# Query and key tiles of an attention layer: products for norm and rotation one gap later, two gaps in every tile, conditioning spread thinner

## The reference, cut to what matters

```python
mod = c_act @ ada_w[i] + ada_b[i]                     # conditioning
sh1, sc1, gt1, sh2, sc2, gt2 = jnp.split(mod, 6, axis=-1)
h = _modulate(_rms(x, norm1_g[i]), sh1, sc1)
...
qkv = h @ w_in
q, k, v = jnp.split(qkv, [ATT_Q_DIM, ATT_Q_DIM + ATT_KV_DIM], axis=-1)
...
q = _rope(_rms(q, q_g).astype(jnp.float32), cos, sin) * (ATT_HEAD_DIM ** -0.5)
k = _rope(_rms(k, k_g).astype(jnp.float32), cos, sin)
...
p = jnp.exp(scores - m)
p = p / (p.sum(axis=-1, keepdims=True) + jnp.exp(sink - m))
o = jnp.einsum('bnhgqk,bnkhd->bnqhgd', p.astype(vb.dtype), vb).reshape(b, s, ATT_Q_DIM)
```

## Time and profile before

| | us |
|---|---|
| median of 3 runs (3039.64 to 3040.81) | 3040.3 |
| the profiled execution | 3037.79 |
| its span, first to last instruction | 3036.0 |
| TensorE busy | 2671.8 (88%) |
| VectorE busy | 1683.7 (55%) |
| ScalarE busy | 930.1 (31%) |
| GpSimd busy | 1242.4 (41%) |
| landing of one qk weight after its issue, median | 5.0 |

### The profile page before, as it was taken

One profiled execution on the slowest core, in us unless ns is written; L12 is line 12 of the kernel. 1 busy time (PEld: TensorE's weight loads), 2 busy tenths in 40 slices (PEclk: granted clock), 3 DMA queues, 4 the chain that ended last, 5 costly groups with the idle time before them and its releaser, 6 DMA issues. The chain is left out here.

```text
span 3036.0 us, 48379 instructions
## 1 busy us (share of the span) xinstructions
PE 2671.8 (88%) x20064; PEld 2192.0 (72%) x20064; DVE 1683.7 (55%) x2078; ACT 930.1 (31%) x1551; POOL 1242.4 (41%) x630
## 2 busy tenths in 40 slices
PE   1787888999999999899996677887789999999999
PEld 1565666888877788677775576776777888878887
DVE  6754545765535543567762788788525543434434
ACT  2435333222223222255442222222234222222221
POOL 2432244444445344443432333334255444444443
PEclk9989998999999999999997888888999999999999
DMA  6421233355522233266675333333142233332333
GB/s 238 160 77 41 84 106 130 134 197 174 172 93 97 84 104 97 84 163 167 156 183 126 83 76 94 70 79 84 35 153 84 97 97 98 97 91 90 104 97 125
DMA packets 299000, 343.31 MB, mean 113 GB/s; under 512 B 214560, under 2 KB 214688, under 8 KB 298784
## 3 DMA queue, kind: packets, MB, share of 16 engines
q1 hardware_dynamic: 298784, 340.23, 37.5%
HBM read 298.29 MB, written 40.89 MB: 112 GB/s over the span
## 5 line engine op out<-in xcount | busy, mean ns | idle before, releaser
L709 POOL TENSOR_TENSOR wl<-w,wh 128x1024 fp32r<-128x1024 f32 x367 | 905.3, 2472 | 1281.2 <-ACT wh L750 1281.1
L180 PE MATMUL ps<-hi,wh 128*128 128x512 f32 x2208 | 883.4, 400 | 22.0 <-ACT qk_raw L787 10.4
L181 PE MATMUL ps<-lo,wh 128*128 128x512 f32 x2208 | 869.1, 394 | 0.0
L182 PE MATMUL ps<-hi,wl 128*128 128x512 f32 x2208 | 868.9, 394 | 0.0
L750 ACT ACTIVATE wh<-w 128x1024 fp32r<-128x1024 f32 x367 | 386.9, 1056 | 706.6 <-DMA w<-in_ffn_w_in 526.1
L1021 DVE SCALAR_TENSOR_TENSOR xt<-ps,mod,xt 128x512 f32<-128x512 f32 x384 | 286.7, 750 | 415.8 <-PE ps L182 407.6
L180 PEld LDWEIGHTS ps<-hi,wh 128*128 128x128 f32 x2208 | 420.4, 190 | 124.7 <-issue 33.8
L181 PEld LDWEIGHTS ps<-lo,wh 128*128 128x128 f32 x2208 | 420.7, 191 | 89.9 <-issue 3.7
L182 PEld LDWEIGHTS ps<-hi,wl 128*128 128x128 f32 x2208 | 420.0, 190 | 90.2
L1026 DVE TENSOR_TENSOR act<-ps,silu 128x512 f32<-128x512 f32 x88 | 60.9, 692 | 459.5 <-PE ps L182 459.5
L180 PE MATMUL ps<-act_hi,wh 128*128 128x512 f32 x704 | 282.3, 401 | 18.3 <-DVE act_lo L1030 10.7
(11 more groups left out here) (221 smaller groups left out, 3389.7 us busy)
## 6 DMA issues: line engine op xcount, KB each, us to landing
w<-in_ffn_w_in SPq DMA_DIRECT2D x176, 512.0 KB, 3.7
piece<-in_ada_w SPq DMA_DIRECT2D x96, 512.0 KB, 4.9
w<-in_ffn_w_out SPq DMA_DIRECT2D x88, 512.0 KB, 3.7
w<-in_w_rkv SPq DMA_DIRECT2D x48, 512.0 KB, 3.9
scratch<-silu SPq DMA_DIRECT2D x48, 256.0 KB, 2.9
scratch<-act SPq DMA_DIRECT2D x48, 256.0 KB, 3.1
w<-in_wqk SPq DMA_DIRECT2D x20, 512.0 KB, 5.0
xt<-in_xT SPq DMA_DIRECT2D x4, 2048.0 KB, 9.9
```

The costliest lines, as they stand in the source:

```text
L180: pe.matmul(out, w_hi(k), x_hi(k), start=first and k == 0, stop=False)
L181: pe.matmul(out, w_hi(k), x_lo(k), start=False, stop=False)
L182: ins = pe.matmul(out, w_lo(k), x_hi(k), start=False, stop=last and k == kc - 1)
L709: pool.tensor_tensor(wl[n % NW][:, :, :], wr[n % NW][:, :, :], wh[n % NW][:, :, :].bitcast(F32), ALU.subtract).then_inc(*wlo.up)
```

## The change

A few lines of the function that lays out the attention layer are changed.

```diff
                 else:
                     head, root, rest = norms[1]
-                    plan.side = joined(spread(head, 6) + [root] + spread(rest, 2), spread(plan.ada_steps(2, 4, 3), 3))
+                    plan.side = joined(spread(head, 3) + [root] + spread(rest, 1), spread(plan.ada_steps(2, 4, 3), 2))
                 for n in range(QCH + KCH):
                     j = (QCH + n) % (QCH + KCH)
-                    if n and plan.side:
-                        plan.side[0] = aux() + plan.side[0]
-                    elif n:
-                        plan.side = [aux()]
-                    plan.tile("qk", h, j, [plan.slot("wqk", j)], cuts=(3, 6) if h else (4,))
+                    if n:
+                        plan.side += [[]] * (2 - len(plan.side))
+                        plan.side[1] = aux() + plan.side[1]
+                    plan.tile("qk", h, j, [plan.slot("wqk", j)], cuts=(3, 6))
                     if h:
                         plan.between()
```

## The result

The changed kernel takes 3042.41 us (median of 20 runs, 3037.58 to 3049.46) against 3039.50 for the kernel before (20 runs): ratio 1.0014, 95% interval 1.0008 to 1.0020. So it is 2.9 us slower, inside the range, on the other side of the forecast of 3.4 us faster.

The account below looks back on a forecast made before the run. VectorE, slowed by GpSimd, was taken to bound the first half, a closed chain across engines the second. First half -4.0 and second half +0.6 gave -3.4 against the 3040.3 median: 3036.9, said as 3037; range 3030 to 3043.

Parts of the forecast that it names:

- First half, -4.0: First half of query and key tiles: v tiles begin at 184.8 instead of 188.8; bounds -12 and -1.
- Leg A: First half, to the start of tile 5: norm's matmul goes from 108.28 to 109.4, tile 5 begins at 119.5.
- Leg B: First half, tile 5 to tile 8: VectorE sets it, loses 7.9 us to GpSimd; tile 8 starts at 160.7.
- rival 1: First half: GpSimd's instructions hold VectorE for their full length, 10.9 us lost; total -0.4, 3039.9; chance 0.18.
- The 0.85: First half: VectorE loses 0.85 us for each us of GpSimd's work it meets, read from a stretched pair of pieces.
- The closed chain, 14.03 to 13.43: Second half's tile time: attention output's remainder, 0.60, leaves the chain; six turns gain 3.6 us.
- The clock, 1.8: Second half: 2.5 us waits ahead of transposes lower TensorE's clock in three tiles of six, costing 1.8 us.
- The entry, +2.4: Second half's first such tile: matmuls and value products run ahead of the products, so the chain starts 2.4 us later.
- The exit, 0: Second half, at the last weighing: TensorE has its fill of work again, no wait moves on, no cost.
- Rival 2: Engines meet in half of GpSimd's work (-4.0) and the clock stays full (-1.8): total -9.2, 3031.1; chance 0.27.
- Rival 3: First half: every conditioning piece meets GpSimd and takes 2.8 us; total +6.9, 3047.2; chance 0.07.
- Rival 4: First half: products of tiles 3 and 5 go behind a conditioning product; two waits of 1.3 us; no own chance.

Follow-up runs that it names:

- second half filled: Kernel with only the second half changed, plus six unread small products in TensorE's wait ahead of the transposes of units 1 to 6; 3.1 us over before.
- values first: Kernel before, with the second half's products of squares and rotation put behind the value products of their gap; 5.8 us under before.
- second trace of before: Kernel before, unchanged, traced a second time; no time of its own given, 362.1 us on the "whole" stretch against 361.8 in the first trace.
- second half alone: Changed kernel's second half with the first half of the kernel before; 2.7 us over before, ratio 1.0002 to 1.0019.
- first half alone: Changed kernel's first half with the second half of the kernel before; 2.9 us under before, ratio 0.9983 to 1.0000.
- after, held: Changed kernel, with GpSimd's remainder held at the entry until two units' maxima are done and at the exit until the last weighing; 1.9 us over before.
- values first, remainder late: Changed kernel's first half; second half's products at the first gap behind value products, GpSimd's remainder behind its tile's weighing and maxima; 3019.7 us, 20.0 under before.
- remainder late: Kernel before, with GpSimd's weight remainder in the second half put behind the weighing and maxima of its tile; 16.0 us under before.

## Why the prediction was wrong

**First half, -4.0: held up, a little too large.** Base to first scores is 131.4 in seven traces with the first half of before and 128.3 in five with that of after: -3.1. Leg A was 0.3 to 1.0 late: tile 2's products came 26.4 behind the base (25.9 worked out), the norm's matmul 37.1 (36.2). Leg B took 41.9 from tile 5 to tile 8 (41.2 worked out): the VectorE instructions that met GpSimd there lost 8.2 us, where 7.9 were worked out and rival 1 had 10.9. By its size, then, the forecast was nearer; by its mechanism rival 1 was. In the traces every VectorE instruction with two inputs in SBUF that begins within a remainder ends behind it. The 0.85 was read from one pair of pieces; that it came out right for leg B, where one of the three cosine products met no such instruction at all, is in part luck.

The Trainium skill (SBUF — State Buffer, section SBUF: two separate sides) calls the pair of ports that VectorE and GpSimd share an exclusive lock, held for a whole instruction. The traces agree: 2.24 for 0.17 us, ending 0.03 behind the remainder; 2.77 for 0.69; 3.07 for 1.22. The instructions that read PSUM, the reciprocals and the row maxima went through at their length. But two inputs aren't needed: the conditioning's first product (L1142 of the kernel before, one tile read) took 2.84 to 2.89 for 0.75 each of the twelve times that it began within a remainder.

**The closed chain, 14.03 to 13.43: right.** With the clock full it is 13.45 from weighing to weighing in six turns on end (second half filled), and 13.5 with values first. By transposes the last turn looks otherwise: before, those of units 1 to 6 stand 1.1 behind the end of their weighing and the last ones right behind theirs, so there the last turn is 13.05. The parts below are therefore counted by weighings, against the second trace of before.

**The clock, 1.8: right in kind and in size.** Three of six waits cost the clock in after, as taken, and two of six in the second half alone; the price in five tiles was 2.4 and 1.2. With it the six turns gave 1.2, where 3.6 less 1.8 was forecast.

**The entry, +2.4: too small.** From the first to the second weighing it takes 15.3 in after and 14.3 in the second half alone, against 11.3: +4.0 and +2.9. The first half alone, with the second half of before, has 12.5 there, at a granted clock of 0.80 behind the first transposes where the second trace of before has 0.88. So some 1.2 of the 4.0 need not be a cost of the later products.

**The exit, 0: this step failed.** The prediction says that where the chain ends "TensorE has its fill of work again and no wait moves on". But the wait that it moved ahead of each group of transposes stands ahead of the last group too, and a remainder of GpSimd now meets the last weighing, which takes 3.07 for 1.22. The last transposes wait 5.71 where they waited 1.71:

```profile
311.25 1.09 PE L954 MATMUL ps<-con,piece 128*128 128x128 f32 x8 [1.71 <-DVE piece L1118]
```

```profile
311.25:342.52 31.27, 31.27 (x178) 25.07 (x178) 9.50 (x14) 10.21 (x15) 13.36 (x7) 1.00 0.35 117
```

Both rows are of before, again: TensorE's last transposes, and the stretch from them to the next scores. In after the clock falls behind the wait. From these transposes to the next scores TensorE has no idle time in either kernel and the same matmuls to do; it takes 33.36 at a granted clock of 0.93, and 31.27 at 1.00: +2.1. With the weighing's +1.8 that is +3.9. Without the remainder's hold (after, held) the wait is still 3.15, the clock still falls, and it takes 34.0 (0.91): +2.7 remain. With the products at the first gap (values first) the clock doesn't fall there. No run filled the wait at the exit, as was done in the tiles.

Against the second trace of before, after is: first half -3.2; first scores to first weighing -0.2; entry +4.0; six turns -1.2; exit +1.8 and +2.1; the rest up to 435 us -0.4. The sum is +2.9, and the medians differ by 2.9. That they agree to a tenth is luck: the profiled execution of after took 3045.89, 3.5 over its median, and what lies behind 435 us takes 2600 to 2605 us in these traces, whatever the kernel.

**The rivals.** Rival 2 (the clock stays full) is out: 0.82 to 0.93 by stretch. Rival 3 (pieces at 2.8 us) is out: the 21 pieces of this kind between 80 and 205 us average 1.59 in after, 1.60 before. Rival 4's price was said to be within legs A and B, and was; what it hid is that products at the first gap would have been 2.2 us better still (125.9 and 126.1, against 128.3). No rival had the exit: the slower one was looked for in the first half. With the working at hand it could have been found: the weighing that was said to be "what is late next" was not followed to the last unit, where the earlier trace rows have the products of tile 8 at 312.25 and TensorE's work around it, and not held against the remainder that GpSimd begins there.

Open is why the wait of 1.89 ahead of the second transposes cost the clock in after and not in the second half alone, and with it how much of the loss another execution would show.

## What to carry to other kernels

A long GpSimd instruction is a hold on VectorE's two-input instructions, and on some with one, wherever it happens to fall. Putting it in a place by a wait is worth something only if that place is one where VectorE has nothing of the kind to do: moved to the wrong place it just took the next step (11.0 for 11.3), or met the rotation's sum in a kernel that lost 25 us; moved beside the exponentials it gave 16.

A chain that runs from tile to tile has a first and a last turn that look different from the others. Walk these two by themselves, since a wait that is moved, and cheap in the turns between, comes out there at full length, and with the clock's price on top.

A single trace can be the lucky one: count from a base behind the last load that varies, and look at whether a step on which the sum rests has 0.1 us to spare.

## What was not expected of the hardware

A VectorE instruction on 128 x 8, 0.17 us long, took 2.24 beside a GpSimd subtraction, and 0.1 us in the landing of one load decided about it.

In the second half, waits of 1.3 to 1.7 us left TensorE's clock at full wherever they were looked at. Of the seven waits of 1.89 us in after and the second half alone, one was followed by the lower level; of the five of 2.63 or 2.64 us, four (in after, held, two of four). And 3.19 us ahead of the first transposes was followed by it at once in one kernel (values first, remainder late) and not at all in another (remainder late, granted clock 1.00 up to the second transposes). So a wait of two to three us has a chance of the lower level, which no trace here turns into a rule; its price was 0.2 to 0.5 us a tile on average, and 2.1 where the longest one stood.
